# A hybrid decoder step in one kernel: where the narrow products, the masks, the last taps and the finish stand

## What is computed

```python
u = xn @ w_in                                   # 1024 x 10272
a = glu_v * sigmoid(glu_g)                      # conformer branch
a = silu(layer_norm(causal_dwconv(a_full, 31 taps) + bias))
y_a = a @ conf_out_w + conf_out_b
xbc = silu(causal_dwconv(xbc_full, 4 taps))     # SSD branch, chunks of 128
y, h = ssd(xs, dt, A, bm, cm, h0)               # masks w = cb * decay, states h
y = rms_norm_by_group((y + d_skip * xs) * silu(z)) * ssm_norm_w
y_b = y @ ssm_out_w
out = (gate_a * y_a + gate_b * y_b) @ w_o       # + residual
moe = top-1 group, top-2 expert of 32 gated MLPs
y = rms_norm(x + out + moe) * norm_final_w
```

## Time and profile before

| | us |
|---|---|
| three runs | 1513.21, 1509.61, 1515.84 (median 1513.21) |
| the profiled execution, its own time | 1508.43 |
| its span | 1506.7 |
| granted clock of TensorE, mean over the span | 0.938 |
| busy: PE, DVE, ACT, POOL | 89%, 76%, 55%, 14% |
| DMA, mean | 181 GB/s |

### The profile page before, as it was taken

One profiled execution on the slowest core, in us unless ns is written; L12 is line 12 of the kernel. 1 busy time (PEld: TensorE's weight loads), 2 busy tenths in 40 slices (PEclk: granted clock), 3 DMA queues, 4 the chain that ended last, 5 costly groups with the idle time before them and its releaser, 6 DMA issues. The chain is left out here.

```text
span 1506.7 us, 25985 instructions
## 1 busy us (share of the span) xinstructions
PE 1344.8 (89%) x8586; PEld 1192.2 (79%) x8586; DVE 1152.1 (76%) x1637; ACT 822.7 (55%) x1468; POOL 212.6 (14%) x328
## 2 busy tenths in 40 slices
PE   6999999999999999999966999996289999999970
PEld 5988889888898888988846899976278777777760
DVE  4688788988888888888874464524669999999955
ACT  5463545546355463544623233312469999999952
POOL 1021120301203021120210000000301111111112
PEclk9999999999999999999968999998599999999995
DMA  6242626244172441716428353305579999999926
GB/s 201 79 113 82 178 70 191 60 138 125 57 193 65 134 120 58 213 49 172 120 69 280 96 161 97 102 26 192 219 299 378 366 365 366 374 373 373 358 98 251
DMA packets 191725, 273.47 MB, mean 181 GB/s; under 512 B 15789, under 2 KB 154245, under 8 KB 175252
## 3 DMA queue, kind: packets, MB, share of 16 engines
q1 hardware_dynamic: 179100, 247.84, 49.6%
q0 software_dynamic: 9536, 17.98, 3.4%
q10 hardware_dynamic: 3040, 7.03, 1.2%
HBM read 237.68 MB, written 52.48 MB: 193 GB/s over the span
## 5 line engine op out<-in xcount | busy, mean ns | idle before, releaser
L914 PE MATMUL pu<-xh,wh 128*128 128x304 f32 (+1 forms) x1280 | 290.0, 309 | 0.1
L914 PE MATMUL pu<-xl,wh 128*128 128x304 f32 (+1 forms) x1280 | 275.1, 297 | 0.0
L914 PE MATMUL pu<-xh,wl 128*128 128x304 f32 (+1 forms) x1280 | 274.5, 296 | 0.0
L914 PEld LDWEIGHTS pu<-xh,wh 128*128 128x128 f32 x1280 | 202.1, 194 | 17.7 <-issue 15.9
L914 PEld LDWEIGHTS pu<-xl,wh 128*128 128x128 f32 x1280 | 203.5, 195 | 0.0
L914 PEld LDWEIGHTS pu<-xh,wl 128*128 128x128 f32 x1280 | 202.2, 194 | 0.0
L1064 DVE SCALAR_TENSOR_TENSOR cacc<-a_p,gc,cacc 128x528 f32<-128x528 f32 x232 | 188.7, 814 | 5.0
L1823 DVE TENSOR_TENSOR W13l<-W,W13h 128x1024 fp32r<-128x1024 f32 x160 | 185.0, 1217 | 4.5 <-issue 4.2
L549 ACT ACTIVATE wh<-ring 128x1024 fp32r<-128x1024 f32 x80 | 84.3, 1054 | 151.5 <-PE pu L914 147.5
L1807 ACT ACTIVATE W13h<-W 128x1024 fp32r<-128x1024 f32 x160 | 156.3, 1064 | 0.2 <-issue 0.2
L2248 PE MATMUL eh<-W13h,xch 128*128 128x512 f32 x320 | 130.2, 407 | 8.7 <-DVE xcl L2347 7.7
(11 more groups left out here) (401 smaller groups left out, 2624.7 us busy)
## 6 DMA issues: line engine op xcount, KB each, us to landing
W<-in_exp_w SPq DMA_DIRECT2D x100, 1024.0 KB, 7.2
ring<-in_w_in SPq DMA_DIRECT2D x80, 512.0 KB, 4.2
x<-in_exp_w SPq DMA_DIRECT2D x20, 1024.0 KB, 7.4
stage<-decay_rows SPq DMA_DIRECT2D x8, 1120.0 KB, 6.7
x<-in_state_ssm SPq DMA_DIRECT2D x16, 512.0 KB, 7.0
out_new_ssm_sample<-x SPq DMA_DIRECT2D x16, 512.0 KB, 7.3
wraw<-in_ssm_out_w SPq DMA_DIRECT2D x8, 1024.0 KB, 6.9
Ed<-decay_rows SPq DMA_DIRECT2D x32, 140.0 KB, 6.9
```

What stands on the lines that cost most here:

```text
L914: last = pe.matmul(u_cols(r, a, b), w[:, k % RING, j, :], x[:, j, a:b], start=(j == 0 and n == 0), stop=(j == KD - 1 and n == 2))
```

## The change

1. In a group of the trunk TensorE runs `samples(0)` one step earlier and `samples(2)` and `samples(3)` one step later, so that whole steps of block 9 stand between the sets.
2. VectorE makes the masks of the first two chunks ahead of the taps that stood before them; two taps move from `stage2(1)` and `(2)` to a place before `stage2(5)`.
3. The last group's ten `trail` taps leave the trunk. SP writes the partial convolution and the gated rows, and VectorE adds the taps in the mixer, behind `low(1)`; the sums over `aconv` wait for them. Behind the loop TensorE sums the squares ahead of `states_added`. SP's order is new, and it loads a third group's rows early, the last group's: it needs no gate on the store, since a semaphore `s_ylast` carries it into the mixer.
4. The finish has no block of its own. Its instructions stand at the end of the experts' programs, in tiles of that block that are free by then. The residual rows and the norm's weights are loaded when the last tile's inputs have been split; the row tile of 32 samples comes last.

```diff
-EARLY = 2
+EARLY = 3
...
-            results_out(G - 1)
             sp.wait_ge(s_hs, 4 * G + 1)
             sp.wait_ge(s_yst, 16 * (G - 1) + 1)
-            for n in range(EARLY):
-                sp.dma_start(early_rows(keep["x1"], n), keep["yrows"][n].rearrange("i p t -> p i t")).then_inc(s_early, 16)
-            conv_out(G - 1)
+            sp.wait_ge(s_part, 1)
+            sp.dma_start(keep["aconv"][G - 1], cacc[:, :]).then_inc(s_part, 16)
+            sp.dma_start(keep["gated"][:, :], a_p[:, :]).then_inc(s_part, 16)
+            early(0)
+            early(1)
+            results_out(G - 1)
+            sp.wait_ge(s_st_h, 32 * G + 1)
+            early(2)
...
                 block(9, 0, 2)
                 states_turned(2)
-                block(9, 2, 4)
+                block(9, 2, 3)
+                samples(0)
+                block(9, 3, 4)
                 states_turned(3)
-                samples(0)
                 block(9, 4, 5)
                 samples(1)
                 block(9, 5, 6)
                 stage2(5)
+                block(9, 6, 7)
                 samples(2)
-                block(9, 6, 7)
+                block(9, 7)
                 samples(3)
-                block(9, 7)
...
+            for r in range(2):
+                squares_summed(G - 1, r)
             for r in range(4):
+                if r < 2:
+                    pe.wait_ge(s_root, 2 * (G - 1) + r + 1)
                 states_added(G - 1, r)
             closing(G - 1)
-            for r in range(2):
-                squares_summed(G - 1, r)
...
                 split(g, 7)
-                taps(3)
                 dve.wait_ge(s_dec, 80 * g + 80)
                 stage1(0)
+                taps(1)
                 stage1(1)
+                taps(2)
                 for j in range(5):
-                    taps(3 if j in (1, 2) else 2)
+                    taps(2)
                     stage2(j)
...
                     split(g + 1, 0)
+                taps(2)
                 stage2(5)
...
             group(G - 1, is_last=True)
-            states_new(G - 1, range(2))
             squares_joined(G - 1)
-            states_new(G - 1, range(2, 4))
-            conf_taps(G - 1, range(CK - TRAIL, CK - 3))
+            states_new(G - 1, range(4))
             scaled(G - 1)
-            conf_taps(G - 1, range(CK - 3, CK))
...
+                if n == KD - 1:
+                    sp.wait_ge(keep["s_ylast"], 16)
                 sp.dma_start(yraw[:, n % YR], keep["yrows"][n].rearrange("i p t -> p i t")).then_inc(s_yr[n % YR], 16)
             sp.dma_start(aconv[:, :, :], keep["aconv"].rearrange("k p t -> p k t")).then_inc(s_ac, 16)
+            sp.dma_start(gated, keep["gated"]).then_inc(s_ac, 16)
...
                 if n == 1:
-                    pe.wait_ge(s_ac, 16)
+                    pe.wait_ge(s_ac, 32)
+                    pe.wait_ge(s_taps, 1)
...
             low(1)
+            dve.wait_ge(s_ac, 32)
+            for j in range(CK - TRAIL, CK):
+                acc = aconv[:, KD - 1, SAMP:T]
+                ins = stt(acc, gated[:, j:j + PROMPT], cs[:, KD - 1, R_CW + j:R_CW + j + 1], acc)
...
+            sp.wait_ge(s_xh, finished(NTILE - 1))
+            sp.wait_ge(s_xl, finished(NTILE - 1))
+            sp.dma_start(x2[:, 1:, :], keep["x1_rows"][SAMP:, :].rearrange("(t p) d -> p t d", p=P)).then_inc(s_x1[1], 16)
+            sp.dma_start(x2[0:SAMP, 0, :], keep["x1_rows"][0:SAMP, :]).then_inc(s_x1[0], 16)
+            sp.dma_start(nf, A["norm_final_w"].partition_broadcast(P)).then_inc(s_nf, 16)
...
             for b in range(2):
                 pool.wait_ge(s_yst[b], 16 * (NTILE // 2))
+            for n, t in enumerate(LAST):
+                S = OT[t][1]
+                for q in range(2):
+                    pool.indirect_dma_start(out=ye[2 * n + q][0:S, :], out_offset=None, in_=keep["ysc"],
...
-        finish(nc, A, O, keep)
```

More of the change, by code:

```diff
@@ L344, in results_out @@
                 sp.wait_ge(s_yn, 2 * g + 2 + 1)
-                sp.dma_start(keep["yrows"][g].rearrange("i p t -> p i t"), yout[:, :, :]).then_inc(s_yst, 16)
+                stored = keep["s_ylast"] if isinstance(g, int) and g == G - 1 else s_yst
+                sp.dma_start(keep["yrows"][g].rearrange("i p t -> p i t"), yout[:, :, :]).then_inc(stored, 16)
             def conv_out(g):
@@ L389, in _, with early @@
                     .then_inc(s_wraw, 16)
-            results_out(G - 1)
+            def early(n):
+                sp.dma_start(early_rows(keep["x1"], n), keep["yrows"][n].rearrange("i p t -> p i t")).then_inc(s_early, 16)
             sp.wait_ge(s_hs, 4 * G + 1)
             sp.wait_ge(s_yst, 16 * (G - 1) + 1)
-            for n in range(EARLY):
-                sp.dma_start(early_rows(keep["x1"], n), keep["yrows"][n].rearrange("i p t -> p i t")).then_inc(s_early, 16)
-            conv_out(G - 1)
+            sp.wait_ge(s_part, 1)
[6 more added lines that the diff above has]
+            early(2)
+            sp.wait_ge(s_part, 33)
             sp.wait_ge(s_early, 16 * EARLY)
@@ L780, in _ @@
             group(G - 1, is_last=True)
-            closing(G - 1)
+            root(G - 1)
+            rows_moved(G - 1)
             act.wait_ge(s_gst, 32 * G + 1)
@@ L890, in squares_summed @@
                 pe.wait_ge(s_sqs, g + 1)
-                pe.wait_ge(s_hnew, 4 * g + 4 + r)
+                if not (isinstance(g, int) and g == G - 1):
+                    pe.wait_ge(s_hnew, 4 * g + 4 + r)
+                else:
+                    pe.wait_ge(s_h0tev, 4 * g + 3 + r)
                 pe.matmul(turn[r][:, 0:280], ones[:, :], th[:, 0, 280 * r:280 * r + 280],
@@ L1435, in mixer @@
         mean, ya = rr, sq
+        gated = mg[:, KD - 1, 0:CK - 1 + PROMPT]
         ss2 = sb("ss2", [P, 8])
@@ L2137, in experts @@
         s_settled = sem("e_settled")
+        pos, wgt = keep["pos"], keep["wgt"]
+        after = xc[:, :, :].rearrange("p k c -> p (k c)")
+        x2 = after[:, 0:NT * D].rearrange("p (t d) -> p t d", t=NT)
+        nf, junk = after[:, NT * D:NT * D + D], after[:, NT * D + D:NT * D + 2 * D]
+        pairs = keep["W13"][:, :, :, :].rearrange("p b a f -> p (b a f)")
+        ye = [pairs[:, D * n:D * n + D] for n in range(8)] + [keep["W2"][0][:, D * n:D * n + D] for n in range(2)]
+        LAST = list(range(1, NT)) + [0]
+        s_nf, s_x2, s_sum, s_var, s_sd, s_out, s_st = map(sem, ("f_nf", "f_x2", "f_sum", "f_var", "f_sd", "f_out", "f_st"))
+        s_ye = [sem(f"f_ye{n}") for n in range(2 * NT)]
+        s_x1, c_dve = [sem(f"f_x1{n}") for n in range(2)], sem("f_dve")
         block = ctx.enter_context(nc.Block())
@@ L2225, in _ @@
                 pool.wait_ge(s_yst[b], 16 * (NTILE // 2))
+            for n, t in enumerate(LAST):
+                S = OT[t][1]
+                for q in range(2):
+                    pool.indirect_dma_start(out=ye[2 * n + q][0:S, :], out_offset=None, in_=keep["ysc"],
+                                            in_offset=bass.IndirectOffsetOnAxis(ap=pos[0:S, NT * q + t:NT * q + t + 1], axis=0))\
+                        .then_inc(s_ye[2 * n + q], 16)
         @block.tensor
@@ L2342, in _ @@
             store(NTILE - 1, 1)
+            act.activation(warm[:, :], ident[:, 0:1], ACT.Sqrt)
+            for n, t in enumerate(LAST):
+                S = OT[t][1]
+                act.wait_ge(s_x2, n + 1)
+                if n:
+                    act.wait_ge(s_sum, n)
+                act.activation(junk[0:S, :], x2[0:S, t, :], ACT.Square, accum_out=ssf[0:S, t:t + 1]).then_inc(s_sum, 1)
+                act.wait_ge(s_var, n + 1)
+                act.activation(ssf[0:S, t:t + 1], ssf[0:S, t:t + 1], ACT.Sqrt).then_inc(s_sd, 1)
         @block.vector
@@ L2465, in combine @@
+            links = Steps(dve, c_dve)
+            def combine(n):
+                t = LAST[n]
+                S = OT[t][1]
+                dve.wait_ge(s_x1[0 if t == 0 else 1], 16)
+                for q in range(2):
+                    dve.wait_ge(s_ye[2 * n + q], 16)
+                    ins = dve.scalar_tensor_tensor(out=x2[0:S, t, :], in0=ye[2 * n + q][0:S, :],
+                                                   scalar=wgt[0:S, q, t:t + 1], in1=x2[0:S, t, :],
                                                    op0=ALU.mult, op1=ALU.add)
@@ L2484, in _ @@
             dve.wait_ge(s_nf, 16)
-            for t in range(1, NT):
-                combine(t)
-                variance(t - 1)
-                if t >= 2:
-                    normalise(t - 2)
+            for n in range(1, NT):
+                combine(n)
+                variance(n - 1)
+                if n >= 2:
+                    normalise(n - 2)
             normalise(NT - 2)
@@ L2507, in program @@
                 "aconv": nc.dram_tensor("conv_rows", (KD, P, T), F32, kind="Internal").ap(),
+                "gated": nc.dram_tensor("gated_rows", (P, CK - 1 + PROMPT), F32, kind="Internal").ap(),
```

(2 more changed lines are left out.)

100 lines of the change are left out of this document (33 added, 67 removed).

## The result

The changed kernel takes 1484.01 us in the median of four runs (1476.80 to 1490.75), the one before 1511.41 (1505.59 to 1515.84), shown beside it: 27 us between the medians, ratio 0.9842, interval 0.9805 to 0.9878. The forecast was 1470 us, in a range of 1457 to 1497. The profiled execution is one of the long ones of the four: 1488.71 us, span 1486.8, 20.0 us less than before's span of 1506.7.

What follows compares the result with a forecast made beforehand. TensorE, busy 89% of the span, was taken as the bound: time only in its waits, low clock or stretches it does not set. Terms -22 -12.5 +6.3 -2.4 -9.5 from 1508.43 gave 1468.3, 1470 for the median; range 1457 to 1497.

Steps and rivals of the forecast that it cites:

- The clock: Trunk loop: spacing narrow products between wide steps removes TensorE's stretches at clock 0.50; -22 us, bound 0 if falls stay.
- the stretch at 272.65: Short low-clock stretch in the trunk, put down to a mask wait, not narrow products; the two short ones cost 1.7 us each.
- The reading of the second group: Trunk: same product order kept clock 1.00 over 6.83 us there, said to be from more wide work around its stage2.
- Masks ahead of taps: Trunk loop: earlier masks cut TensorE's waits from 3.4 to 1.8 us a group; -12.5 us over eight groups, bounds 0 and 27.
- The end of the trunk: Block 9 to the mixer's start: longer, 35.5 us instead of 29.2, squares ahead of states; +6.3 us, bounds +2 and +10.
- The mixer: Mixer: first product's last operand and the split of weight 1 come earlier; -2.4 us (0 to -4), ten taps cost nothing.
- The ten taps: Mixer: 8 us of moved taps end at 30 us, TensorE asks at 31.5; no cost, cover 1.5 us.
- The finish: End of kernel: gathers start soon after the last scatter, VectorE ends 11.8 us earlier, block end adds 2.4; -9.5 (-6.5 to -11).
- the 1468.3 of the sum: Whole kernel: five terms totalling -40.1 us against the profiled execution's 1508.43; 1470 given for the median.

Runs made afterwards that it cites:

- e1: Kernel before with only the new order of the narrow products (the samples sets); 1500.38 us, ratio 0.9950.
- e2: Kernel before with only the new order of masks ahead of taps; 1487.52 us, ratio 0.9853.
- e5: Changed kernel with its four sets of narrow products directly behind one another, behind step 6 of block 9; 1484.71 us, ratio 0.9844.
- e7: Changed kernel, taps still in the mixer, but states ahead of squares, two states ahead of VectorE's last three taps, two early loads; 1472.83 us, ratio 0.9785.
- e8: Changed kernel with 16 unread matmuls added, 14 at the mixer's end and two at the route's start; 1481.81 us, ratio 0.9821.
- e10: e9 with the 16 unread matmuls of e8 around the route added; 1468.81 us, ratio 0.9738 to the kernel before.
- e124: Changed kernel with the old end of the trunk and start of the mixer, so parts 1, 2 and 4 alone; 1479.14 us, ratio 0.9797.
- e6: Changed kernel with samples(0) alone put back where it was, behind the last turn of the states; 1476.32 us, ratio 0.9789.
- e9: Changed kernel with the edits of e6 and e7 together; 1465.17 us, ratio 0.9735 to the kernel before.
- e11: Changed kernel again, unedited, for a second profile and more runs; 1483.62 us, ratio 0.9855 to the kernel before.
- e4: Kernel before with only the finish moved into the experts' block; 1500.09 us, ratio 0.9939.

## Why the prediction was right, and where it was off

The sign and the range held; the forecast of 1470 was 14 us too low.

**The clock.** That the stretches behind the samples would go held, and the sum was near: at the lower clock the trunk lost 22.5 us before, behind its start-up and up to the end of block 9 of the last group, and it loses 1.7 in the changed kernel's profile (the stretch from 170.92). The cause was given by half. The step said that the order of the narrow products does it alone, 22 us. Counted the same way, as half of the time at 0.50, the loss is 12.0 us with the products alone (e1) and 12.7 with the masks alone (e2): each part wins about 10, and only the two together leave 1.7. So the sum came out near with the help of a part to which the step gave nothing, and that is luck.

The runs show two kinds of falls: behind a wait for the first mask (e1; early masks take these away), and behind narrow products while TensorE is busy throughout (e2, e5). The text had seen the first kind (the stretch at 272.65 "follows a wait for the mask") and counted it as an exception. The stretch that is left goes with a wait as well. Of the eight profiles that have the products apart and the masks early, five have a wait of 1.75 to 2.96 us for a split weight in the second group (changed, e7, e8, e10, e124), and each of them has a stretch at 0.50 that begins in that wait or right behind it, at 170.68 to 175.18; the other three (e6, e9, e11) wait at most 1.2 us there and have none.

The reading of the second group, on which the term leaned, was wrong. Its products do not stand in more wide work. Before, its sets were as close as in the group of the earlier trace rows, and the third stood behind the small `stage2(5)` with no step between, as at 671.00 there:

```profile
210.31 0.95 PE L968 MATMUL pC<-cv,x 128*128 128x4 f32 x8
...
211.97 0.95 PE L968 MATMUL pC<-cv,x 128*128 128x4 f32 x8
...
214.07 1.05 PE L968 MATMUL pC<-cv,x 128*128 128x4 f32 x8
```

Why this group, and two of the waits in e1, had no fall behind them, the runs don't settle, nor why the stretch was 6.83 us long before and 3.41 with early masks.

The Trainium skill's page "TensorE: Matmul & The Clock Gate" puts falls down to idle gaps ("Why this matters for your kernels"); the prediction set that against the rows and took the rows. e1 agrees with the page in kind only: the falls stand behind a wait, but one of 1.78 us, and the page's row is on longer gaps. e5 does not agree, with falls at 100% busy.

**Masks ahead of taps.** The wait that stays, 1.8 us a group, was right in size, though it is two waits for `hT` of 0.9 and 0.5 us where the step had one of 1.3 and another ahead of `samples(0)`. The gain of 1.6 us was taken for all eight groups, 12.5. Alone (e2) the part takes 11.9 us from TensorE's idle time over the seven turns of the loop (each from the first mask's product of a group to that of the next); in the changed kernel it is 9.1, since the first and the third of them gained only 0.8 and 0.5. Of the 2.8 us between the two, 2.1 lie in the first turn, the one with the wait of 1.95 us for `wl`. What the step left out is worth nearly as much: the shorter waits also bring the loss at the lower clock from 22.5 to 12.7 us (e2), so that this part alone gives 22 us. The parts overlap: products, masks and finish give 9, 22 and 9 alone, and 30 together (e124), not 40. Some of that gap is not theirs: the experts' matmuls, which no edit touches, take 379.3 us in e124's profile and 374.8 to 375.2 in the other three.

**What no step held.** Narrow sets between wide steps cost TensorE 0.4 us a group, 3 us in all; most of that is `samples(0)`, whose move wasn't needed (e6).

**The end of the trunk.** It is 10.4 us to the first `states_added` (about 10) and 35.5 to the mixer (35.5). That the last came out to the tenth is luck: the third early load is issued 29.4 us behind block 9 where 28 were forecast, and the mixer follows it by 6.1 us where 7.5 were. That this part lost, as it was made, is shown by e124's pieces, and by e7 that the order and the third load are what lost.

**The mixer.** -1.1 instead of -2.4, within its bounds. The split of weight 1 ends 19.9 us behind the mixer's first issue, where it was 21.3: 1.4 earlier, not 2.4. The ten taps are covered: TensorE's waits in the mixer are for `yl` and `vl` alone, 22.2 and 0.9 us (in e6 0.8 and in e7 1.2 us are for the taps).

**The finish.** -8.4 instead of -9.5, and two errors stand against each other in it. VectorE's last row ends 29.73 us behind the last scatter's issue instead of 38.05, so 8.3 earlier where 11.8 were forecast. The terms that were mis-sized are the gathers: the first is issued 2.9 us behind the scatter (2.2 taken) and lands in 4.4 (3.5 taken), and VectorE then waits for others four times, 2.1 us in all; the ten land in a median of 5.5 us. The bounds of 2.1 and 6.4 held this. On the other side, the 2.4 us of a block's end at the very end do not come: from the last row to the end of the span it is 3.5 us now and was 3.6. From the Trainium skill's page "DMA: Bandwidth & Descriptors" (section "Anatomy of one DMA — SWDGE (gpsimd) path") came an estimate of 3.2 us for a transfer of 512 KB by itself; the first here took 4.4, and the seven of that size behind it 5.1 to 6.4.

**What was not looked at.** The route was taken as unchanged. It takes 24.6 or 32.6 us from one execution to the next of the same kernel (e11 and the changed kernel's first profile), and the profile of before had a short one (57.9 us from the mixer's last matmul to the experts' first); none of the rows read was of the route. The changed kernel's first profile is the only one of the eleven without added matmuls that has a long one, so how often it comes, and whether it makes all the upper runs, is not shown. That execution, at 1488.71 us, lies 20.4 above the 1468.3 of the sum: 8.6 are the trunk to the end of block 9, 8.1 the route, the rest mixer, experts and finish. The one of e11, at 1478.91, lies 10.6 above: 6.9 are the trunk to the end of block 9, and none the route.

## What to carry to other kernels

When a clock falls in a busy stretch, look for a wait in the same period as well: here either cure alone left about half of the loss at the lower clock, and only the two together took nearly all of it. A step moved off a busy engine is no gain by itself; at the trunk's end the order in which the results came free set the time. With the taps moved and the squares first the end was 4 us longer than before the move (e124), and with the states first and one load less 12 us shorter than that, of which 3 came back in the mixer (e7). Compare pieces of a span rather than spans: pieces that no edit touches differed by 8 us between two executions. A term that comes out to the tenth may be two errors that cancel; check its parts.

## What was not expected of the hardware

A chain of small products has two speeds with nothing changed but the execution: the route's 124 matmuls take 24.6 us at a mean granted clock of 0.71 or 32.6 at 0.50. TensorE comes to it behind 5.5 us of idling, and when the clock comes back up early, as from 1017.31 to 1027.55 in e11, 82 of the 124 matmuls run at the upper level. With 14 wide matmuls behind the mixer and two ahead of the route it was up at once in both profiles that had them (24.2 us, 0.82 and 0.84), hardly less than the 24.6 of the short route without them.

The time of the experts' products, too, goes with their start: it is 373.4 and 373.6 us in the two profiles with no stretch at 0.50 behind their first transposes (e6, e7), 374.8 to 375.3 in the four with one of 3.41 us (e1, e2, e4, e9), 377.3 to 381.1 in those with two or a longer one (e124 and e8 have a further one near the end). No edit was made to test it.
